# Norm passes round the output product in another order, three row buffers, routing in two goes

## The reference

```python
y_lat, y_ctx = token_mixer(modulate(x, ...), modulate(xc, ...), ...)   # ends in m @ w_out + b_out
x   = layer_norm(alpha * x + g_a * y_lat, ln1_g[l], ln1_b[l])
h_f = modulate(x, sh_f, sc_f)                    # a second norm, times (1 + scale), plus shift
# hier_moe(h): the best of 4 groups, in it the best 2 of 8 experts, by a softmax of h @ w_rg and h @ w_re
#   out[token] = sum over its two experts of weight * (silu(h @ w_gate) * (h @ w_up)) @ w_down
x = layer_norm(alpha * x + g_f * f_lat, ln2_g[l], ln2_b[l])
```

## Time and profile before

| | |
|---|---|
| median of 3 runs | 2760.17 us (2758.97 to 2762.04) |
| the profiled execution | 2761.03 us, its span 2759.2 us |
| busy share: TensorE, VectorE, ScalarE, GpSimd | 91%, 33%, 23%, 13% |
| chain that ended last: TensorE, DMA, VectorE | 70%, 13%, 8% |
| mean DMA rate over the span | 219 GB/s |

### The profile page before, as it was taken

One profiled execution on the slowest core, in us unless ns is written; L12 is line 12 of the kernel. 1 busy time (PEld: TensorE's weight loads), 2 busy tenths in 40 slices (PEclk: granted clock), 3 DMA queues, 4 the chain that ended last, 5 costly groups with the idle time before them and its releaser, 6 DMA issues.

```text
span 2759.2 us, 33032 instructions
## 1 busy us (share of the span) xinstructions
PE 2511.6 (91%) x12815; PEld 1551.8 (56%) x12815; DVE 921.2 (33%) x1708; ACT 627.0 (23%) x1172; POOL 349.8 (13%) x409
## 2 busy tenths in 40 slices
PE   5999899999999899989986999899999998989984
PEld 3769566788884543434332768567886443433331
DVE  3344566522224820001005534556332630000003
ACT  2321344522210111111102321446331000111110
POOL 1231000001111220000102430000011211000001
PEclk8999999999999899999998999999999999999997
DMA  9571001322217679999996560004333789999994
GB/s 286 195 246 46 6 1 13 87 58 69 58 43 224 254 309 420 421 421 419 420 420 234 186 210 25 7 1 87 92 99 127 266 345 419 420 420 404 420 421 165
DMA packets 238331, 604.39 MB, mean 219 GB/s; under 512 B 67328, under 2 KB 143504, under 8 KB 188640
## 3 DMA queue, kind: packets, MB, share of 16 engines
q1 hardware_dynamic: 210786, 528.65, 50.8%
q0 software_dynamic: 24512, 63.13, 6.5%
q10 hardware_dynamic: 2880, 10.49, 0.9%
HBM read 585.70 MB, written 38.16 MB: 226 GB/s over the span
## 4 chain that ended last, share of the span: by engine, by line
PE 70%; DMA 13%; DVE 8%; ACT 3%; SPq 3%; issue 2%; POOL 0%; ACTq 0%; DVEq 0%; POOLq 0%
PE slot L1079 20%; PE abank L677 18%; PE vbank L677 11%; DMA arena<-in_w_up_e 6%; PE slot L983 5%; DMA arena<-in_w_down_e 3%; DMA arena<-in_w_gate_e 2%; PE vbank L859 2%; SPq L2569 2%; DVE nmx L1491 1%; DMA arena<-in_w_in 1%; PE slot L886 1%; PE abank L757 1%; PE vbank L669 1%; PE vbank L806 1%
## 5 line engine op out<-in xcount | busy, mean ns | idle before, releaser
L1079 PE MATMUL slot<-arena 128*64 128x512 f32 (+2 forms) x3264 | 825.6, 613 | 82.5 <-DMA arena<-in_w_up_e 56.8
L1079 PEld LDWEIGHTS slot<-arena 128*64 128x64 f32 (+2 forms) x3264 | 295.7, 146 | 558.9 <-issue 548.7
L677 PE MATMUL abank<-round,round 128*128 128x512 f32 (+1 forms) x1792 | 492.6, 356 | 11.9 <-DVE round L1556 8.3
L677 PEld LDWEIGHTS abank<-round,round 128*128 128x128 f32 x1792 | 319.6, 190 | 74.9 <-issue 19.1
L1798 DVE TENSOR_TENSOR arena<-slot,arena 128x512 f32<-128x512 f32 x76 | 52.5, 691 | 801.0 <-ACT arena L2102 510.8
L677 PE MATMUL abank<-hT_low,round 128*128 128x512 f32 (+1 forms) x896 | 319.1, 356 | 0.0
L677 PE MATMUL vbank<-round,round 128*128 128x512 f32 (+2 forms) x1312 | 307.2, 360 | 1.8 <-issue 1.7
L677 PEld LDWEIGHTS vbank<-round,round 128*128 128x128 f32 x1312 | 227.0, 189 | 37.4 <-issue 3.4
L677 PEld LDWEIGHTS abank<-hT_low,round 128*128 128x128 f32 x896 | 169.6, 189 | 23.7
L1582 DVE TENSOR_TENSOR arena<-vbank,arena 128x512 f32<-128x512 f32 x72 | 43.4, 603 | 307.0 <-PE vbank L677 307.0
L983 PE MATMUL slot<-arena 128*128 128x512 f32 x320 | 140.1, 599 | 3.4 <-POOL arena L2265 3.4
(11 more groups left out here) (284 smaller groups left out, 2769.1 us busy)
## 6 DMA issues: line engine op xcount, KB each, us to landing
arena<-in_w_gate_e SPq DMA_DIRECT2D x128, 1024.0 KB, 26.0
arena<-in_w_up_e SPq DMA_DIRECT2D x128, 1024.0 KB, 26.9
arena<-in_w_down_e SPq DMA_DIRECT2D x128, 1024.0 KB, 28.1
arena<-in_w_ada POOLq DMA_DIRECT2D x80, 512.0 KB, 5.0
arena<-in_w_in SPq DMA_DIRECT2D x48, 512.0 KB, 4.2
arena<-in_w_in SPq DMA_DIRECT2D x8, 2048.0 KB, 14.4
h_rows<-arena ACTq DMA_DIRECT2D x20, 512.0 KB, 6.5
arena<-y_rows SPq DMA_DIRECT2D x20, 512.0 KB, 7.9
```

The costliest lines, as they stand in the source:

```text
L677: last = pe.matmul(to, x, y, start=(k == 0 and q == 0), stop=(k == len(terms) - 1 and q == 2))
L1079: last = pe.matmul(to[at, cols], x[:, at], w[:, at_w, :], start=first, stop=final)
```

## The change

VectorE runs, for each n: residual(n), modulated(n-1) (the second norm), affine(n) (the first norm), logits(n-3); for the last tile modulated(n-1) stands ahead of residual(n), and logits of three more tiles surround modulated(last). Working tiles go from three to two, row tiles h8 from two to three. ScalarE's queue has router_rows(n-2) behind store_rows(n), with the last store behind all copies. The best two are taken in two goes: all tiles but the last, then logits(last) and the last alone. The first expert's rows are copied out ahead of the places. SyncE issues the input rows behind b_re (the context rows stay in front), and residual() waits for its own tile's input row only. TensorE's last routers stand with fewer fillers between them. GpSimd's deviations follow VectorE's order.

```diff
@@ -960,7 +970,7 @@
                         ps = act()
                         for q in range(4):
                             k = 4 * half + q
-                            last = pe.transpose(ps[:, q * P:(q + 1) * P], h8[n % 2][:, k * P:(k + 1) * P], ident)
+                            last = pe.transpose(ps[:, q * P:(q + 1) * P], h8[n % 3][:, k * P:(k + 1) * P], ident)
                         close(last, agroups)
                     mark["h8_used", L, n] = st["g"]
                     pe.wait_ge(act_taken, len(agroups))
@@ -996,13 +1006,12 @@
                     if n >= 3:
                         router(n - 3)
                 spare = slot[len(qt) % 2]
-                router(len(qt) - 3)
-                pe.wait_ge(slot_taken_v, before(L) + len(qt) - 1)
-                keep_clock(spare, 4)
-                router(len(qt) - 2)
+                for n in range(len(qt) - 3, len(qt)):
+                    if n == len(qt) - 1:
+                        pe.wait_ge(slot_taken_v, before(L) + n)
+                        keep_clock(spare, 3)
+                    router(n)
                 keep_clock(spare, 3)
-                router(len(qt) - 1)
-                keep_clock(spare, 6)
 
                 pe.wait_ge(route_v, 2 * L + 1)
                 ps = vec()
...
+                def affine(n):
...
+                def modulated(n):
...
+                    if n >= 3:
+
+                        dve.wait_ge(h_out[n % 3], stored(L, n % 3) + 32 * (n // 3))
+                        dve.wait_ge(groups_done, mark["h8_used", L, n - 3])
...
+                last = nq - 1
+                for n in range(nq):
+                    if n == last:
+                        modulated(n - 1)
+                    residual(n)
+                    if 0 < n < last:
+                        modulated(n - 1)
+                    affine(n)
+                    if n >= 3:
+                        logits(n - 3)
+                logits(last - 2)
+                modulated(last)
                 logits(nq - 2)
...
+                link(best_two(0, nq - 1))
+                logits(nq - 1)
+                best_two(nq - 1, nq).then_inc(route_v, 1)
@@ -1733,6 +1766,12 @@
                 link(dve.tensor_reduce(xe[0:NE, 0:1], n5, AX_X, ALU.add))
                 dve.tensor_scalar(xe[0:NE, 4 + NX:4 + NX + P], ones[0:NE, :], xe[0:NE, 0:1], None, ALU.mult
                                   ).then_inc(blocks_ready, 1)
+
+                def rows_taken(i):
+                    ps = take()
+                    dve.tensor_copy(xT[i % 3][:, 0:4, :].rearrange("p a b -> p (a b)"), ps[:, :]).then_inc(vec_taken, 1)
+
+                rows_taken(0)
 
                 def each(row):
                     return row.unsqueeze(1).to_broadcast([P, nq, NE])
@@ -2077,11 +2115,21 @@
                         ps = take()
                         act.copy(hTt[n % 2][:, 4 * half:4 * half + 4, :].rearrange("p a b -> p (a b)"), ps[:, :]
                                  ).then_inc(act_taken, 1)
-                for n, t in enumerate(qt):
+
+                def store_rows(n):
+                    t = qt[n]
                     act.wait_ge(hrow_ready, before(L) + n + 1)
                     for k in range(2):
-                        act.dma_start(h_d[k * TOK + t * P:k * TOK + (t + 1) * P, :], h8[n % 2]).then_inc(h_out[n % 2], 16)
+                        act.dma_start(h_d[k * TOK + t * P:k * TOK + (t + 1) * P, :], h8[n % 3]).then_inc(h_out[n % 3], 16)
+
+                last = len(qt) - 1
+                for n in range(last):
+                    store_rows(n)
+                    if n >= 2:
+                        router_rows(n - 2)
+                for n in range(last - 2, last + 1):
                     router_rows(n)
+                store_rows(last)
                 act.wait_ge(route_v, 2 * L + 1)
                 nq = len(qt)
                 act.activation(lg[:, 0:nq, 0:NG], lg[:, 0:nq, 0:NG], ACT.Exp)
@@ -2265,11 +2313,8 @@
                             pool.tensor_tensor(dst, dst, sg[n % 2][:, 0:nn], ALU.add).then_inc(pool_sum, 1)
                             st["sum"] += 1
                         n += 1
-                deviation(mv[:, qt[0], 1:2], rstd[:, qt[0]:qt[0] + 1])
-                for n, t in enumerate(qt):
-                    if n + 1 < nq:
-                        u = qt[n + 1]
-                        deviation(mv[:, u, 1:2], rstd[:, u:u + 1])
+                for t in qt:
+                    deviation(mv[:, t, 1:2], rstd[:, t:t + 1])
                     deviation(mv2[:, t, 1:2], rstd2[:, t:t + 1])
 
                 def names(i):
@@ -2416,10 +2461,9 @@
                              ).then_inc(first_in[j], 16)
 
             def load_x():
-                load_ctx()
                 for b in range(GRID_W // BCOL):
                     sp.dma_start(x_sb[64 * (b % 2):64 * (b % 2) + 64, CTX_TILES + b // 2, :], grid_block(a["x"], b)
-                                 ).then_inc(x_in[0], 16)
+                                 ).then_inc(x_in[1 + b // 2], 16)
 
             mod_rest(0)
             for n in range(DEPTH):
@@ -2527,13 +2571,7 @@
                 for v_ in range(2):
                     mod_row(rows[f"ga{v_}"], v_, 2).then_inc(rows7_in, 16)
                 if L == 0:
-                    load_x()
-                else:
-                    for t in qtiles(L):
-                        sp.wait_ge(x_in[t - 1], 48)
-                    for t in qtiles(L):
-                        sp.dma_start(x_sb[:, t, :], x_d[(t - CTX_TILES) * P:(t - CTX_TILES + 1) * P, :]
-                                     ).then_inc(x_in[0], 16)
+                    load_ctx()
                 broadcast(rows["ln_g"], a["ln1_g"][L]).then_inc(rows8_in, 16)
                 broadcast(rows["ln_b"], a["ln1_b"][L]).then_inc(rows8_in, 16)
                 for v_ in range(2):
@@ -2546,6 +2584,14 @@
                                  ).then_inc(rows8_in, 16)
                     broadcast(brow[:, 0:NG], a["b_rg"][L]).then_inc(rows8_in, 16)
                     broadcast(brow[:, NG:36], a["b_re"][L]).then_inc(rows8_in, 16)
+                if L == 0:
+                    load_x()
+                else:
+                    for t in qtiles(L):
+                        sp.wait_ge(x_in[t - 1], 80)
+                    for t in qtiles(L):
+                        sp.dma_start(x_sb[:, t, :], x_d[(t - CTX_TILES) * P:(t - CTX_TILES + 1) * P, :]
+                                     ).then_inc(x_in[t - 1], 16)
                 wgf = a["w_gate_e"].rearrange("l e d f -> (l e d) f")
                 wuf = a["w_up_e"].rearrange("l e d f -> (l e d) f")
                 wdf = a["w_down_e"].rearrange("l e f d -> (l e f) d")
```

More of the change, by code:

```diff
@@ L478, in before, with stored @@
             return sum(len(qtiles(k)) for k in range(L))
+        def stored(L, b):
+            return sum(32 for k in range(L) for n in range(len(qtiles(k))) if n % 3 == b)
         def RB(L, stage):
@@ L1624, in _ @@
                     link(dve.scalar_tensor_tensor(T, x_sb[:, t, :], mv2[:, t, 0:1], rows[f"sc{c}"],
                                                   ALU.subtract, ALU.mult))
[L1626 to L1630, removed]
-                    dve.scalar_tensor_tensor(h8[n % 2], T, rstd2[:, t:t + 1], rows[f"sh{c}"], ALU.mult, ALU.add
-                                             ).then_inc(hrow_ready, 1)
@@ L1633, in _ @@
-                    if n >= 2:
-                        logits(n - 2)
+                    dve.wait_ge(rstd_ready, RB(L, "s8") + out_norm2(n))
+                    if n >= 3:
+                        dve.wait_ge(h_out[n % 3], stored(L, n % 3) + 32 * (n // 3))
+                        dve.wait_ge(groups_done, mark["h8_used", L, n - 3])
+                    dve.scalar_tensor_tensor(h8[n % 3], T, rstd2[:, t:t + 1], rows[f"sh{c}"], ALU.mult, ALU.add
+                                             ).then_inc(hrow_ready, 1)
@@ L1635, in _ @@
+                last = nq - 1
[10 more added lines that the diff above has]
+                modulated(last)
                 logits(nq - 2)
-                logits(nq - 1)
-                dve.wait_ge(vec_taken, st["v"])
@@ L1664, in _ @@
-                for n in range(nq):
-                    last = dve.tensor_tensor(
-                        q32[:, n, :].rearrange("p (a b) -> p a b", a=NG), e[:, n, :].rearrange("p (a b) -> p a b", a=NG),
-                        r4b[:, n, :].unsqueeze(2).to_broadcast([P, NG, EG]), ALU.add)
-                link(last)
-                link(dve.tensor_reduce(s1[2], q32, AX_X, ALU.max))
-                first(oh[:, 0, 0:nq, :], q32, s1[2], i32, NE, q32b, s1[1])
-                link(dve.scalar_tensor_tensor(q32, oh[:, 0, 0:nq, :], 2 * NEG, q32, ALU.mult, ALU.add))
@@ L1785, in _ @@
                     part, i, half = step
-                    if part == "rows":
-                        ps = take()
-                        dve.tensor_copy(xT[i % 3][:, 0:4, :].rearrange("p a b -> p (a b)"), ps[:, :]).then_inc(vec_taken, 1)
```

(10 more changed lines are left out.)

74 lines of the change are left out of this document (46 added, 28 removed).

## The result

The changed kernel takes 2776.91 us (median of 4 runs, 2775.99 to 2778.13), the kernel before 2759.57 beside it: 1.0066 times as long, interval [1.0053, 1.008]. That is 17.3 us more where 7.2 were forecast, and 0.9 us above the upper end of the range. The direction was right, the size was not.

What follows compares the result with a forecast made beforehand. TensorE was taken as the bound for most of the span; any microsecond ahead of the first expert product counts in full. +9.6 + 4.0 - 1.9 - 3.9 - 0.6 = +7.2 us gave 2767.4, range 2765.7 to 2776.

Steps and rivals of the forecast that it cites:

- The copies on ScalarE decide: Block one: router(0)'s and router(1)'s copies wait behind stores of later row tiles, holding TensorE 8.8 and 8.0 us.
- Affine(0): First norm of block one: starts at 862 once the norm rows are loaded, bounds 860.1 and 871.0.
- Its waits for GpSimd: Block one's norms: only tiles 4 and 5 keep the 0.8 us wait, and affine(5) gets one.
- +4.0 for two: Block one: slow clock after each of two TensorE waits costs 2.0 us, bounds 1.5 and 2.7.
- The clock in block two: Block two: with the slow clock router(3) is done at 2203 to 2205; choices at 2208.6, -3.9 us.
- now comes before nothing but routers and fillers: Block two: TensorE's 5.6 us wait before router(0)'s copies, with no output product behind it.
- The tail of block one: Last row tile to choices: first go 954.4 to 961.0, second to 965.5, plus 0.3 correction.
- Splitting costs nothing much: Block one's best two: two goes end at 965.5, undivided at 966.8.
- Rows ahead of places: First expert's rows copied before the places: -1.9 us in block one, -0.6 in block two.
- Rival 3: Norm rows come later than 862: at 865 the sum is +10, at 871 +16, 2776; no chance of its own.
- Rival 1: Block one: the copies don't hold TensorE, so the sum is -14.0 and the time 2746; 12%.

Runs made afterwards that it cites:

- experiment 1: Changed kernel with ScalarE's router copies one store behind instead of two: 2751.43 us, 0.9966 times the kernel before.
- Experiment 3: Changed kernel with filler products inside TensorE's waits for the copies (8 in each of block one's two, 5 in block two): 2768.48 us, 1.0037 times the kernel before.
- 10: Kernel of Experiment 9 with the best two taken in one go instead of two: 2752.80 us, 0.9969 times the kernel before.
- experiment 7: Kernel of experiment 1 with the best two taken in one go behind the last tile's logits: 2757.64 us, 0.9988 times the kernel before.
- experiment 4: Kernel before with only the first expert's rows copied out ahead of the places: 2759.64 us, 0.9993 times the kernel before.
- Experiment 9: Kernel of experiment 1 without three fillers ahead of the last router and with logits(last-3) ahead of affine(last): 2744.01 us, 0.9938 times the kernel before.
- 5: Kernel of experiment 1 without the three fillers ahead of the last router: 2745.14 us, 0.9944 times the kernel before.
- 6: Kernel of experiment 1 with logits(last-3) ahead of affine(last), the three fillers kept: 2748.03 us, 0.9959 times the kernel before.

## Why the prediction was right and wrong

**The copies on ScalarE decide: right.** Router(0)'s product started 65.0 us behind the block's start, forecast 65.6. Each wait delays TensorE by 8.2 us (8.95 less the usual 0.73), where the working gave 8.8 and 8.0. The chain, the 66.12 us of ScalarE's idle time ended by L1645, and experiment 1 show it. Affine(0) started at 861.0, forecast 862; SyncE issued b_re at 857.44. (The working's terms for that mark add up to 861.3, not 861.8.) VectorE waits 15.08 and 13.56 us for the products of tiles 4 and 5 (L1610 at 918.58 and 948.30), as said. Its waits for GpSimd are 0.83 us at affine(5) as said, and 0.52 at modulated(5) and none at modulated(4), where 0.8 was said for both. From the last output product to the last row tile it took 13.5 us, forecast 13.4.

**The clock: the step that failed.** The term "+4.0 for two" was too small. It was taken as 2.0 us for each wait, from the earlier trace rows, which are stretches behind other waits. Measured are (3.6 - 2.0) + (15.3 - 13.8) = 3.1 and (3.6 - 2.0) + (16.3 - 13.8) = 4.1 us, 7.2 instead of 4.0; with the start 0.6 early the last product ends 6.6 behind the forecast's 107.0. The way of reckoning was sound: half of the time that the clock stays at 0.50 once TensorE works again. In the three stretches of the earlier trace rows that time was 3.9, 5.5 and 3.1 us (back at 1506.4, 2294.8 and 2482.6), which gives the text's bounds of 1.5 and 2.7. Here it was 6.4 and 8.4 us, and half of these is 3.2 and 4.2. Three samples behind other work were taken for the whole range. The Trainium skill's rule (TensorE: Matmul & The Clock Gate, Part 1) that activity releases a throttled default spoke for a surcharge, and the trace agrees (0.50 behind both waits); the size was only to be had from a trace.

**The clock in block two: the same step, and the larger miss.** The text saw the wait (5.6 us; it was 4.74) and let router(3) be done at 2203 to 2205, that is 80 to 82 us behind the start. It was done at 86.9. With the last row tile exact (74.8 for 74.9), choices came 16.9 us behind it instead of 10.8: +6.1. It allowed little for the half clock, which held for 20 us, over three routers and the fillers. Experiment 3 gives 5.6 of the 6.1 back by fillers that keep the clock up for routers(0) and (1). It was wrong that the wait "now comes before nothing but routers and fillers", as if that were cheap: the last router is on the path.

**The tail of block one.** From the last row tile to choices 14.3 us, forecast 11.5 with its 0.3 of correction: +2.8. Router(4)'s bank, which waits for logits(2) behind affine(5), was nowhere in the sum (2.47 us), and nothing was allowed for the fillers at half clock, where they take 5.45 us instead of 2.82.

**"Splitting costs nothing much": the gain was far too small.** The text's own ends, 965.5 with two goes and 966.8 undivided, say that splitting saves 1.3 us. Experiments 7 and 10 show 4.9 and 4.2 us from the last row tile on in block one. The text had the last router on time. That router was late in every variant with two goes, and the first go filled the wait; with one go TensorE stood for the choices as well, and counted the places at half clock in experiment 7.

**Rows ahead of places: right in block one** (-1.8 for -1.9, experiment 4), nothing in block two for -0.6.

**The sum.** Block one missed by +5.6, block two by +6.6; 2.3 us were given back elsewhere (3.9 between the blocks, less 0.7 and 0.9): 9.9, which is 17.1 less 7.2. Rival 3's price for the norm rows wasn't due, as these came early; the range reached 2776 by it, and the clock used it up. Rival 1 described a kernel whose copies don't hold TensorE, at 2746. That kernel is experiment 1, at 2751.4: it gains 9 us where rival 1 had 14, as its choices of block one come at 118.7 and not 114.7. Experiment 9 comes to 2744.0 by mending a tail that rival 1's sum didn't hold, so that nearness is luck.

**What stays open.** Why the clock held at half for 20 us in block two and for 10 and 14 in block one; why it fell in experiment 1 behind a wait of 0.73 us; and what of the 3.9 us between the blocks is the clock and what the weight stream.

## What to carry to other kernels

Before delaying a copy or an issue in an in-order queue, write down what each entry ahead of it waits for, and whether that needs the very engine that waits for the copy; here moving the copies one store forward was worth 25 us, where the whole change without the fault gains 9. Price a wait of TensorE at its length plus half of the time that the granted clock stays at 0.50 once TensorE works again. In these two kernels that was 3.1 to 8.4 us with mostly 128x512 products behind the wait and 20 us with short router products, so take a range and not a mean. Fillers help while TensorE would stand, and cost where the next product on the path queues behind them: put them in the wait, not ahead of the last router.

## What the hardware showed that was not expected

- In block two the granted clock fell to 0.50 at 2199.7, just after router(0)'s product had begun behind 4.74 us of standing. It stayed there until 2220.2, while TensorE was busy 18.65 of 20 us with short router products and fillers. In block one it fell while TensorE stood (895.8 and 923.2) and was back at 906.1 and 936.8, with 128x512 products running.
- A long wait isn't needed. The same project(4), behind a wait of 0.73 us, takes 13.98 us in the kernel before and in experiments 7 and 10, and 15.6 to 15.7 in experiments 1, 4, 5, 6 and 9, and in experiment 1 the granted clock was 0.50 from 893.9 to 897.3. The edits don't reach that far up, so the same instructions can have it or not, and why stays open.
- At that clock everything stretches, not only large products: router product 3.63 us for 1.98, eight transposes 1.95 for 1.04, three fillers 5.45 for 2.82, L1022 2.29 for 1.25.
- Unchanged parts of two executions differ by 1 to 3 us at a mark (choices at 122.3 before and 125.5 in experiment 4), and the profiled executions of experiments 9 and 10 stand in the other order (2750.1 and 2747.4) than their medians (2744.0 and 2752.8). A single trace shows where the time lies, not a gain of a few microseconds.
